# Three head-projection chunks of each layer by seven products, and where GpSimd's weight sums start

## What is computed

```python
def hybrid_layer(x, ...):
    h = rms_norm_2(x, norm1_g)
    proj = h @ w_in                      # 1024 -> 10312 columns
    q, k, v, iq, ik, iw, a_in, c_in, g_in = jnp.split(proj, IN_SPLITS, axis=-1)
    ...
    y_attn = dsa_attention(q, k, v, iq, ik, iw) @ w_attn_out
    ...
    merged = gates[:, :, 0] * y_conf + gates[:, :, 1] * y_attn + gates[:, :, 2] * y_sc
    x = x + merged @ w_o
    u = causal_dwconv(rms_norm_2(x, norm2_g) @ w_up, ffn_conv_w) + ffn_conv_b
    u_gate, u_val = jnp.split(u, 2, axis=-1)
    return x + (jax.nn.silu(u_gate) * u_val) @ w_down
```

## Time and profile before

| | us |
|---|---|
| median of 3 runs | 2558.53 (2557.46 to 2559.01) |
| the profiled execution | 2560.35 |
| its span | 2558.0 |
| TensorE busy | 2371.4 (93%) |
| VectorE busy | 1001.5 (39%) |
| ScalarE busy | 482.6 (19%) |
| GpSimd busy | 301.8 (12%) |

### The profile page before, as it was taken

How to read it: one execution, slowest core, us unless ns; L and a number is a source line. 1 busy time by engine, 2 the same in 40 slices (tenths; PEclk the granted TensorE clock), 3 DMA queues, 4 the chain that set the end, 5 groups by cost and what they waited for, 6 DMA issues and landing times.

```text
span 2558.0 us, 32171 instructions
## 1 busy us (share of the span) xinstructions
PE 2371.4 (93%) x12592; PEld 1588.9 (62%) x12592; DVE 1001.5 (39%) x2427; ACT 482.6 (19%) x1069; POOL 301.8 (12%) x260
## 2 busy tenths in 40 slices
PE   6999999699984886998799999999999999998999
PEld 3465544334322453333358888889975888887984
DVE  1256432410103453132326883155311688414540
ACT  2223321211113331211112122012100112201210
POOL 0000000000001001000000004047200000402740
PEclk9999999799997997998899999999999999998999
DMA  8403389589994526999644434445444444443543
GB/s 272 137 33 116 134 304 344 207 302 365 380 377 173 181 89 221 355 378 387 230 152 134 147 132 138 159 132 165 157 156 136 132 136 146 147 159 105 166 156 107
DMA packets 293254, 501.81 MB, mean 196 GB/s; under 512 B 22896, under 2 KB 115312, under 8 KB 293104
## 3 DMA queue, kind: packets, MB, share of 16 engines
q1 hardware_dynamic: 282336, 474.39, 53.5%
q0 software_dynamic: 4096, 14.16, 1.8%
q10 hardware_dynamic: 6672, 11.21, 1.2%
HBM read 489.63 MB, written 10.09 MB: 195 GB/s over the span
## 4 chain that ended last, share of the span: by engine, by line
PE 87%; DVE 4%; DMA 3%; SPq 3%; issue 1%; DVEq 1%; ACT 1%; ACTq 0%; POOL 0%; POOLq 0%
PE bank L3149 25%; PE bank L3172 10%; PE bank L3135 5%; PE bank L698 4%; PE bank L1152 3%; PE bank L3296 3%; PE bank L3304 3%; PE bank L1994 3%; PE bank L2006 3%; PE bank L2573 2%; PE bank L2424 2%; PE bank L732 2%; DMA ring<-in_ada_w 2%; PE bank L286 2%; PE bank L1183 2%; SPq L577 1%
## 5 line engine op out<-in xcount | busy, mean ns | idle before, releaser
L3149 PE MATMUL bank<-hT,ring 128*128 128x256 f32 x2176 | 488.9, 383 | 7.9 <-DVE hT L3508 7.9
L3149 PEld LDWEIGHTS bank<-hT,ring 128*128 128x128 f32 x2176 | 412.7, 192 | 67.1 <-DVE hT L3508 6.6
L3629 DVE SCALAR_TENSOR_TENSOR y_conf<-y_glu,s_cw,y_conf 128x256 f32<-128x256 f32 x480 | 195.0, 478 | 0.8
L3135 PE MATMUL bank<-ring,hT 128*128 128x512 f32 (+1 forms) x320 | 120.7, 540 | 6.1 <-DVE hT L3508 6.1
L3172 PE MATMUL bank<-hT,ring 128*128 128x128 f32 x960 | 113.7, 275 | 0.0
L3172 PEld LDWEIGHTS bank<-hT,ring 128*128 128x128 f32 x960 | 110.6, 192 | 0.1
L3869 POOL TENSOR_TENSOR y_sacc<-y_cx,s_sw 128x512 f32<-128x512 f32 x24 | 29.1, 1214 | 661.1 <-DVE y_conf L3629 658.0
L3135 PEld LDWEIGHTS bank<-ring,hT 128*128 128x128 f32 x320 | 57.1, 194 | 70.2 <-issue 68.3
L1994 PE MATMUL bank<-ring,hT 128*128 128x384 f32 (+1 forms) x224 | 88.9, 540 | 0.0
L2006 PE MATMUL bank<-ring,hT 128*128 128x384 f32 (+1 forms) x224 | 88.8, 539 | 0.0
L871 DVE TENSOR_TENSOR hidA<-sgT,bank 128x256 f32<-128x256 f32 x16 | 6.7, 421 | 198.6 <-ACT sgT L824 86.9
(11 more groups left out here) (617 smaller groups left out, 3621.1 us busy)
## 6 DMA issues: line engine op xcount, KB each, us to landing
extra<-in_exp_w SPq DMA_DIRECT2D x72, 1024.0 KB, 13.0
ring<-in_exp_w SPq DMA_DIRECT2D x72, 1024.0 KB, 14.0
ring<-in_ada_w SPq DMA_DIRECT2D x24, 2048.0 KB, 10.0
ring<-in_w_in SPq DMA_DIRECT2D x24, 2048.0 KB, 7.7
ring<-in_w_up SPq DMA_DIRECT2D x44, 1024.0 KB, 7.0
ring<-in_w_in SPq DMA_DIRECT2D x32, 1024.0 KB, 7.7
spare<-in_exp_w SPq DMA_DIRECT2D x24, 1024.0 KB, 12.9
h_tok<-in_exp_w SPq DMA_DIRECT2D x18, 1024.0 KB, 13.1
```

Of the source, the lines that this page charges most:

```text
L3135: mm = pe.matmul(pair(s)[i][:, 0:qkv_w[c]], h[:, k, i * P:(i + 1) * P], w[:, k, :], start=(k == 0), stop=(k == KT - 1))
L3149: mm = pe.matmul(b, w[:, k, j * P:(j + 1) * P], moving(k), start=(k == 0), stop=(k == KT - 1))
L3629: ins = dve.scalar_tensor_tensor(conf[:, f, :], src, cw[:, f, k:k + 1], conf[:, f, :], ALU.mult, ALU.add)
```

## The change

The head projection's chunks 1 to 3 are now done by `seven_products` too, in both layers; chunk 0 and the narrow chunk 4 stay with `token_products`. VectorE makes the mixtures of h right after the first norm of a layer as well, and the new `head_rows` adds the parts up straight into `qkv` (seven additions a chunk). ScalarE's copies of chunks 1 to 3 give way to `keep_first`. GpSimd makes the sums of three chunks at the head of a layer: chunk 3's wait for chunk 1's products; chunks 1 and 2's wait for the mixtures in layer 1 and only for their weights in layer 0. In the `up` stage chunk 1's sums, which waited for `at` chunk 1, now wait for the mixtures. The counts of `freed_act` are renumbered, and what waited for the copy of `qkv` chunk 3 waits for its last addition.

```diff
--- before.py
+++ after.py
@@ -2911,9 +2911,9 @@
         def order(kind):
-            of = {"qkv": 0, "cb": 5, "g": 7, "a": 0, "c": 4, "at": 8, "sc": 10, "cf": 12}
+            of = {"qkv": -3, "cb": 2, "g": 4, "a": 0, "c": 4, "at": 8, "sc": 10, "cf": 12}
             return of[kind]
-        ACT_KINDS, ACT_N, DVE_KINDS, DVE_N = ("qkv", "cb", "g"), 13, ("a", "c", "at", "sc", "cf"), 14
+        ACT_KINDS, ACT_N, DVE_KINDS, DVE_N = ("qkv", "cb", "g"), 10, ("a", "c", "at", "sc", "cf"), 14
         def sig(name):
             return ctx.enter_context(nc.semaphore(f"y_{name}"))
@@ -2941,7 +2941,7 @@
         sums_made, halves_mixed, part_full, first_kept, mixed = [
             s.sem for s in (run_shared, run_values_full, key_full, run_exp, run_weighed)]
         sm0, hm0, pf0, fk0, mx0 = [s.n for s in (run_shared, run_values_full, key_full, run_exp, run_weighed)]
-        by_seven = [("up", c) for c in range(1, 11)]
+        by_seven = [("qkv", c) for c in range(1, 4)] + [("up", c) for c in range(1, 11)]
         seven = [(l, s) for l in range(2) for s in by_seven]
         PARTS, MIXES = 6, 7
         stretches = list(dict.fromkeys(kind for kind, c in by_seven))
@@ -2995,6 +2995,8 @@
         def freed_at(l, s):
             kind, c = s
+            if s == ("qkv", 3):
+                return mixed, all_mixed(l, s)
             if kind in ACT_KINDS:
                 return freed_act, ACT_N * l + order(kind) + c + 1
             if kind in DVE_KINDS:
@@ -3322,8 +3324,10 @@
                         if j in steps(s):
                             attention_step(l, steps(s)[j])
                     return put
-                for c in range(5):
-                    token_products(l, ("qkv", c))
+                token_products(l, ("qkv", 0))
+                for c in range(1, 4):
+                    seven_products(l, ("qkv", c), h)
+                token_products(l, ("qkv", 4))
                 for kind in ("a", "c", "cb", "g"):
                     for c in range(dict(kinds)[kind]):
                         products(l, (kind, c), lambda k: h[:, k, :], beside((kind, c)))
@@ -3458,8 +3462,10 @@
             squares(0, range(8))
             norm(0)
             for l in range(2):
-                for c in range(5):
-                    keep(l, ("qkv", c))
+                keep(l, ("qkv", 0))
+                for c in range(1, 4):
+                    keep_first(l, ("qkv", c))
+                keep(l, ("qkv", 4))
                 act.wait_ge(qk_squared, l + 1)
                 act.activation(stats[:, 1, 0:20], stats[:, 0, 0:20], ACT.Sqrt, scale=1.0 / HD_C, bias=eps_col[:, :])\
                     .then_inc(qk_root, 1)
@@ -3736,6 +3742,25 @@
                 dve.wait_ge(full, full_at(l, s))
                 dve.tensor_tensor(dst, two_tiles(part_bank(7 * q + 6)[:, 0:256]), other, ALU.add).then_inc(mixed, 1)
+            def head_rows(l, c):
+
+                s = ("qkv", c)
+                q = seven.index((l, s))
+                low_first, high_first, low_second, high_second = [
+                    two_tiles(qkv[:, i, c * COLS + 256 * half:c * COLS + 256 * half + 256])
+                    for i in range(LT) for half in range(2)]
+                dve.wait_ge(first_kept, fk0 + q + 1)
+                add_part(q, 1, low_first, p_one)
+                add_part(q, 2, u_two, p_one)
+                dve.drain()
+                add_part(q, 3, u_three, u_two)
+                dve.drain()
+                add_part(q, 4, high_second, u_three)
+                add_part(q, 4, u_four, u_two)
+                dve.drain()
+                add_part(q, 5, high_first, u_four)
+                add_last(l, s, low_second, u_three)
+
             def up_rows(c):
                 b = [two_tiles(bank[2 * (c % 2) + half][:, :]) for half in range(2)]
@@ -3787,6 +3812,10 @@
             dve.wait_ge(pool_made.sem, pads_zero)
             norm(0, 0)
             for l in range(2):
+                mix_halves(h)
+                for c in range(1, 4):
+                    head_rows(l, c)
+                dve.drain()
                 prepare_index(l)
                 prepare_heads(l)
                 before, k = None, 0
@@ -3857,6 +3886,9 @@
             pool.drain()
             pool.sem_inc(pool_made.sem, 1)
             for l in range(2):
+                for c in range(1, 4):
+                    sem, value = (full, full_at(l, ("qkv", 1))) if c == 3 else (halves_mixed, mixed_at(l, "qkv"))
+                    sum_weights(l, ("qkv", c), sem, value if l or c == 3 else None)
                 sw = small[l]["sw"]
                 sem, value = freed_at(l, ("c", 3))
                 pool.wait_ge(sem, value)
@@ -3876,7 +3908,10 @@
                 pool.sem_inc(short_done, 1)
                 for c in range(1, 11):
                     s = ("up", c)
-                    sum_weights(l, s, full, full_at(l, ("at", 1) if c == 1 else ("sc", 1) if c == 2 else ("up", c - 2)))
+                    if c == 1:
+                        sum_weights(l, s, halves_mixed, mixed_at(l, "up"))
+                    else:
+                        sum_weights(l, s, full, full_at(l, ("sc", 1) if c == 2 else ("up", c - 2)))
         st.end()
         @block.sync
```

## The result

| | us |
|---|---|
| median after, 4 runs | 2535.95 (2532.99 to 2538.28) |
| median before, 4 runs | 2558.64 (2557.46 to 2559.01) |
| ratio | 0.9912, 95% interval 0.9898 to 0.9927 |
| the profiled execution after | 2538.28, span 2536.0 |

A forecast was written before the change was run, and what follows sets the result against it. TensorE, busy 93% of the span, was taken as the bound, with its few standstills. Head-projection chunks (9.9 us) and the `up` norms (10.1 us) sum to 20.0 us off 2558.5: 2538.5 us, range 2534 to 2547.

The forecast's parts named there:

- Head-projection chunks: Head projection, three chunks of each layer by seven products: 12.09 us a chunk instead of 13.73, 9.9 us saved for six.
- Product 2 in layer 1's head and in the `up` stages: GpSimd's first three sums are done 12.9 us after TensorE's start, before product 2 needs them; slack 6 us, cost nothing.
- Layer 0's unguarded sums: Layer 0's head: sums start at 1266.9, norm ends at 1267.0; mixtures beside sums take 2.84 us; cost nothing.
- the rival: Layer 0's head: the sums catch the norm, at up to 7.7 us; 2546.2 us, chance 0.08.
- The norms: Line 3508 at 3.3 us in all four norms; removing GpSimd's collision in the `up` stages gains 10.1 us.
- The two ways: From the last addition to x to `up` 1: 20.7 us in layer 0 and 22.0 in layer 1, before 23.07 and 29.69.
- the other bound named: Both `up` stages keep the longer stretch at the lower clock, 6 us: 1.2 us more each, gain 2.4 smaller.
- Where layer 0's collision cost time: Layer 0's `up` stage: line 3508 takes 5.35 us beside GpSimd's sums, 3.26 without; layer 0 gains 2.4 us.
- The sum: Whole kernel: 9.9 us from the head projection plus 10.1 from the `up` stages, 20.0 us saved.
- The rival of a free norm: The norm stays as slow, since what held line 3508 was not GpSimd; 2548.6 us, chance 0.06.
- GpSimd becomes the bound: At product 2 of 26 chunks, sums of 3.5 us cost 1.5 us a chunk; 2577.5 us, chance 0.03.
- Additive parts: Gains of the head projection, 9.9 us, and of the `up` stages, 10.1 us, simply added.

The follow-up runs named there:

- the late sums: Changed kernel with five more GpSimd additions between the mixtures and the first sums of each `up` stage: 2553.6 us.
- the test: Changed kernel with six GpSimd additions at the very start of the second block, beside layer 0's first norm: 2547.7 us.
- the repeats of the two kernels: Kernel before and changed kernel, each run again unedited: medians 2559.8 us and 2536.9 us.
- the guard alone: Kernel before with one edit, GpSimd's first `up` sums wait for the mixtures: 2547.9 us, ratio 0.9969.
- reads against writes: Changed kernel with extra GpSimd work beside the `up` norms: six additions, which read SBUF, 2544.9 us; eleven memsets, which only write it, 2536.5 us.
- products alone: Changed kernel with GpSimd's first `up` sums waiting for `at` chunk 1 again, as in the kernel before: 2542.1 us, ratio 0.9944.
- two runs of four norms each: Changed kernel with small TensorE products in the norm gaps, 2530.8 us; the same with layer 0's first sums also waiting for the mixtures, 2532.3 us.

## Why the prediction was right, step by step

- *Head-projection chunks.* 12.09 us forecast, 36.26 / 3 = 12.09 measured; 9.9 us for six. Stationary tokens make no difference, and seven additions at 0.42 us a chunk stay far from the path.
- *Product 2 in layer 1's head and in the `up` stages.* Slack of 6 us forecast. Measured from the third sum's end to product 2: 6.1 us in layer 1's head (1914.2 and 1920.3), 7.4 and 5.8 in the `up` stages, and the late sums show it from the other side (4.9 us free, 12.4 us not).
- *Layer 0's unguarded sums.* The first began at 1264.85, 0.15 us before line 3514's end at 1265.0, and held the mixtures to 2.66 to 2.83 us, as forecast; all were made by 1276.0, 5 us before product 2. The hair's breadth was right, and that the sums fell on the right side of it was luck as much as forecast; but what hung on it was 12.5 us in the test and not 7.7: the rival had its chance from two landings of one trace and its price from three held steps, where eight can be.
- *The norms.* Line 3514 at 3.25 and 3.26 us, as forecast. The two ways, 20.7 and 22.0 us forecast, are 21.92 and 20.28. Layer 0's is 1.2 longer, since its half-clock stretch stayed at 6 us (the other bound named), and layer 1's 1.7 shorter, since the clock didn't fall at all there, which the sum had not allowed for. The two errors cancel, by luck: 42.2 against 42.7 us.
- *Where layer 0's collision cost time.* The forecast gave line 3508's 5.35 us as the sign of it. But TensorE never waited for that held step: the first chunk takes 16.96 us in the kernel before and 16.95 in the changed one, without a wait for a tile in either. All of the 23.07 - 21.92 = 1.15 us lies ahead of line 3508, where VectorE's last addition of squares, which has two inputs in SBUF too, stood beside a sum. Before, then after:

```profile
1679.31 1.57 DVE L3520 TENSOR_TENSOR hT<-hT 128x256 f32<-128x256 f32 x1
```

```profile
1672.42 0.42 DVE L3526 TENSOR_TENSOR hT<-hT 128x256 f32<-128x256 f32 x1
```

In layer 1 the same addition went from 1.43 to 0.43 us, and the rest of the 29.69 - 20.28 = 9.41 us is the held steps of line 3508 and the lower clock around them.
- *The sum.* 20.0 us forecast. The second block's time fell by 20.0 in the traces and by 21.0 in the repeats of the two kernels (1293.9 against 1272.9); the medians by 22.7 and 19.2. In the first pair the parts are 4.9 and 5.0 us in the two head projections and 1.15 and 9.41 in the two `up` stages, less 0.4: in layer 1's head projection line 3514 began 0.4 us later after the reciprocal than line 3508 had, for which the trace names no wait, and whose cause stays open. The 2 us between the medians and these figures fit the drift of the first block, which the forecast could not see and the range took in.
- *The rival of a free norm.* That the norm stays slow for another reason is excluded by the guard alone and by reads against writes. That GpSimd becomes the bound at its speed here is excluded by the late sums: even 12.4 us late it didn't pass the delay on.
- *Additive parts.* The forecast took the two gains as independent. They are not quite: products alone gave 14.0, the guard alone 8.2, both 19.2 us. The total was right all the same, because each term was the kernel before less a state that both changes together reach: chunks at 12.09 us and clean norms.

## What to carry to other kernels

Before GpSimd is given work, look for VectorE instructions with two inputs in SBUF on the critical path beside it, count them, and multiply by one GpSimd instruction each: eight short steps took 3.3 us alone and 20 us beside a stream of readers. That is VectorE's price; ask next whether the engine behind it waits, since a single held step in layer 0's `up` stage cost TensorE nothing. Where the collision hangs on when weights land, a wait on the event that ends the critical part costs nothing as long as it delays the work by less than the slack behind it, so count that first. And where TensorE stands idle for some 3 us at a norm, small products into an unused bank keep its clock up: here they took 5.6 us off three restarts.

## What the runs showed of the hardware that I had not expected

- VectorE's instructions with two inputs in SBUF and GpSimd's readers took turns: one step of 0.41 us between two GpSimd instructions of 2.3 to 2.5 us, 19.96 us for eight, in the one run with such a stream. GpSimd loses little, up to 2.8 us an instruction beside the mixtures instead of 2.35.
- GpSimd's start 0.15 us later or sooner against the norm moved line 3514 by a whole held step of 2.1 us (3.26 against 5.35), though not, in that place, the time of the kernel.
- After gaps of TensorE of 2.5 to 3.4 us at these norms the granted clock stayed up, or was at the lower level for 3 to 4 or for 6 to 7 us, and one program run twice differed at the same place; with 0.3 to 0.7 us left of the gap it never fell in two runs of four norms each.
